# A two-block transformer kernel: table sets named ahead of ScalarE's loops, logarithms and exponentials grouped, experts' transposes in transpose mode

## What is computed

```
def rmsnorm(x, g):
    return x * rsqrt(mean(x * x, -1) + EPS) * g

# first block: norm, projection, two chunked scans over both directions (GLA and mLSTM), then
gla_o = head_rmsnorm(gla_h, g1) * silu(gg)
ml_o = sigmoid(mo) * head_rmsnorm(ml_h, g2)
x = x + g1x * (concatenate([gla_o, ml_o]) @ w_out)
# hierarchical mixture of experts: 32 experts, 2 per token, rows sorted by expert, blocks of 128 rows
def expert_block(xb, e):
    gate, up = split(xb @ e_w_in[e])            # 1024 -> 2 x 512
    return (silu(gate) * up) @ e_w_out[e]       # 512 -> 1024
x = x + g2x * hier_moe(modulate(rmsnorm(x, norm2_g), sh2x, sc2x))
# second block: two layers of mixers (HGRN2 scan, dilated windows, RWKV7), twice a convolved GLU FFN,
# a gated embedding: sigmoid(rmsnorm(h) @ ple_gate) * ..., a last norm
q = silu(q_raw); f = lb + (1 - lb) * sigmoid(f_raw); log_f = log(f)     # HGRN2
```

## Time and profile before

| | before |
|---|---|
| median of 3 runs | 5431.38 us (5431.25 to 5441.96) |
| profiled execution: span | 5435.4 us |
| around the span | the runs' median is 4.0 us below it |
| TensorE busy, matmuls | 4075.4 us, 75% |
| VectorE busy | 2548.6 us, 47% |
| ScalarE busy | 1390.1 us, 26% |
| GpSimd busy | 113.4 us, 2% |
| DMA | 603.89 MB, mean 111 GB/s |
| experts' stage | 878.27 us of the span |

### The profile page before, as it was taken

How to read it: one execution, slowest core, us unless ns; L and a number is a source line. 1 busy time by engine, 2 the same in 40 slices (tenths; PEclk the granted TensorE clock), 3 DMA queues, 4 the chain that set the end, 5 groups by cost and what they waited for, 6 DMA issues and landing times. The chain is left out here.

```text
span 5435.4 us, 55977 instructions
## 1 busy us (share of the span) xinstructions
PE 4075.4 (75%) x18901; PEld 3193.1 (59%) x18902; DVE 2548.6 (47%) x3659; ACT 1390.1 (26%) x1865; POOL 113.4 (2%) x188
## 2 busy tenths in 40 slices
PE   7698811689774998888479844563897779899877
PEld 2487711568553777766358733441785557777756
DVE  1211156446532745777421146656443357567543
ACT  0401021210213755777320021112002032001022
POOL 0000000000001000000100000000000000000000
PEclk9899955877786999999689977676777889999989
DMA  6132114323362856888323210012001122222211
GB/s 245 54 93 79 55 50 135 108 74 96 127 232 107 316 195 233 312 317 310 110 73 97 81 47 32 24 23 89 26 26 41 46 66 85 83 83 86 83 56 45
DMA packets 438154, 603.89 MB, mean 111 GB/s; under 512 B 50477, under 2 KB 314692, under 8 KB 437828
## 3 DMA queue, kind: packets, MB, share of 16 engines
q1 hardware_dynamic: 370072, 459.47, 25.8%
q10 hardware_dynamic: 51552, 86.52, 4.6%
q0 software_dynamic: 16464, 57.07, 2.8%
HBM read 470.13 MB, written 132.84 MB: 111 GB/s over the span
## 5 line engine op out<-in xcount | busy, mean ns | idle before, releaser
L1577 DVE TENSOR_TENSOR exp_w_lo<-exp_w_raw,exp_w_hi 128x1024 fp32r<-128x1024 f32 x384 | 450.4, 1222 | 174.3 <-ACT exp_w_hi L1551 171.6
L1551 ACT ACTIVATE exp_w_hi<-exp_w_raw 128x1024 fp32r<-128x1024 f32 x384 | 381.9, 1050 | 130.1 <-DMA exp_w_raw<-in_expert_w_in 129.7
L324 PE MATMUL in_ps_psum<-hN_hi,in_wh 128*128 128x512 f32 x768 | 301.3, 392 | 52.1 <-DVE in_wl L318 52.1
L324 PE MATMUL up_ps_psum<-hN_hi,up_wh 128*128 128x512 f32 x704 | 285.7, 406 | 70.9 <-DVE up_wl L318 40.6
L325 PE MATMUL in_ps_psum<-hN_lo,in_wh 128*128 128x512 f32 x768 | 300.9, 392 | 0.0
L326 PE MATMUL in_ps_psum<-hN_hi,in_wl 128*128 128x512 f32 x768 | 300.3, 391 | 0.0
L325 PE MATMUL up_ps_psum<-hN_lo,up_wh 128*128 128x512 f32 x704 | 280.6, 399 | 0.0
L326 PE MATMUL up_ps_psum<-hN_hi,up_wl 128*128 128x512 f32 x704 | 280.2, 398 | 0.0
L324 PE MATMUL exp_up_psum<-exp_w_hi,exp_x_hi 128*128 128x512 f32 x592 | 241.8, 409 | 35.3 <-DVE exp_w_lo L1577 34.9
L316 DVE CAST in_wh<-in_w 128x1024 fp32r<-128x1024 f32 x48 | 33.3, 695 | 461.6 <-PE in_ps_psum L326 450.5
L325 PE MATMUL exp_up_psum<-exp_w_lo,exp_x_hi 128*128 128x512 f32 x592 | 232.4, 392 | 0.0
(11 more groups left out here) (653 smaller groups left out, 9129.5 us busy)
## 6 DMA issues: line engine op xcount, KB each, us to landing
exp_w_raw<-in_expert_w_in SPq DMA_DIRECT2D x256, 512.0 KB, 5.1
exp_w_raw<-in_expert_w_out SPq DMA_DIRECT2D x128, 512.0 KB, 5.8
up_w<-in_ffn_up SPq DMA_DIRECT2D x88, 512.0 KB
moe_rows<-zero_rows ACTq DMA_DIRECT2D x50, 512.0 KB, 2.7
ada_w<-in_ada_w SPq DMA_DIRECT2D x12, 2048.0 KB, 7.8
in_w<-in_w_in SPq DMA_DIRECT2D x48, 512.0 KB, 4.0
down_w<-in_ffn_down SPq DMA_DIRECT2D x44, 512.0 KB
exp_rows<-moe_rows POOLq DMA_DIRECT2D x39, 512.0 KB, 6.2
```

Of the source, the lines that this page charges most:

```text
L324: pe.matmul(out, r(w[0]), r(x[0]), start=start, stop=False)
L1551: act.activation(wh[:, c, :].bitcast(F32R), raw[r][:], ACT.Copy).then_inc(s_wh, 1)
L1577: dve.tensor_tensor(wl[:, c, :].bitcast(F32R), raw[r][:], wh[:, c, :], ALU.subtract).then_inc(s_wl[r], 1)
```

## The change

Three things:

- `act.preload_act_table_set(name)` is written ahead of ScalarE's loops (and of the groups of logarithms and exponentials), and names the one set that the loop uses: silu for conv, experts and the up projection, exp for gla, sigmoid for the embedding, and for the gates and hgrn a set that has both Ln and Exp.
- In `stage_norm`, `stage_join` and the RWKV exit all logarithms come first and then all exponentials, where before each Ln was followed by its Exp. In the two-part join VectorE's adds of a part are issued together, ahead of that part's products. Semaphore targets follow.
- In `stage_experts` the turns of the rows and of `h` are `pe.transpose` and no longer `pe.matmul` against the identity.

```
--- before.py
+++ after.py
@@ -354,11 +354,13 @@
                         if n >= NB:
                             act.wait_ge(s_used, n - NB + 1)
                         act.activation(sq[n % NB][:], at(src, h, k), ACT.Square).then_inc(s_sq, 1)
+                act.preload_act_table_set("natural_log")
                 for h in range(nh):
-
                     act.wait_ge(s_used, 8 * h + 8)
                     act.activation(rstd[h][:], pm[h][:], ACT.Ln, bias=K.c("eps")).then_inc(s_rt, 1)
-                    act.wait_ge(s_rt, 2 * h + 1)
+                act.preload_act_table_set("exp_and_others")
+                for h in range(nh):
+                    act.wait_ge(s_rt, nh)
                     act.activation(rstd[h][:], rstd[h][:], ACT.Exp, scale=-0.5).then_inc(s_rt, 1)
                     for k in range(8):
                         n = 8 * h + k + 1
@@ -395,7 +397,7 @@
                 for n in range(8 * nh):
                     h, k = n // 8, n % 8
                     if k == 0:
-                        dve.wait_ge(s_rt, 2 * h + 2)
+                        dve.wait_ge(s_rt, nh + h + 1)
                     if parts and n >= NB:
                         dve.wait_ge(s_lo, n - NB + 1)
                     if shift is not None:
@@ -745,6 +747,7 @@
 
             @block.scalar
             def _(act):
+                act.preload_act_table_set("natural_log_exp_and_others")
                 act.wait_ge(s_lb, NCH)
                 act.activation(le[:], lx[:], ACT.Abs).then_inc(s_a, 1)
                 act.wait_ge(s_a, 1)
@@ -828,6 +831,7 @@
 
             @block.scalar
             def _(act):
+                act.preload_act_table_set("silu_and_others")
                 with act.Fori(0, D // P // NU) as i:
                     for u in U:
                         act.wait_ge(s_tap[u], (i + 1) * NTAP)
@@ -1178,10 +1183,12 @@
                     dve.tensor_tensor(a[u][:], a[u][:], b[u][:], ALU.add).then_inc(s_x[u], 1)
                 heads = [(r, u) for r in range(len(parts)) for u in U]
                 if two:
-                    add(0, 0)
+                    for u in U:
+                        add(0, u)
                 for n, (r, u) in enumerate(heads):
-                    if two and n + 1 < len(heads):
-                        add(*heads[n + 1])
+                    if two and u == 0 and r:
+                        for v in U:
+                            add(r, v)
                     dve.wait_ge(s_a[u], r * 3 + 3)
                     step = Count(dve, s_v[u], r * 2)
                     step(dve.scalar_tensor_tensor(rs[u][:], rs[u][:], K.col(parts[r][1], u), g[u][:], ALU.mult, ALU.mult))
@@ -1190,16 +1197,23 @@
             @block.scalar
             def _(act):
                 for r in range(len(parts)):
+                    steps = [Count(act, s_a[u], r * 3) for u in U]
+                    act.preload_act_table_set("natural_log")
                     for u in U:
                         if two:
                             act.wait_ge(s_x[u], r + 1)
                         else:
                             act.wait_ge(s_in[u], (r + 1) * nin)
-                        step = Count(act, s_a[u], r * 3)
-                        step.mark(act.activation(sq[u][:], a[u][:], ACT.Square))
+                        steps[u].mark(act.activation(sq[u][:], a[u][:], ACT.Square))
+                    for u in U:
                         act.wait_ge(s_mm[u], r + 1)
-                        step(act.activation(rs[u][:], pm[u][:].rearrange("p a b -> p (a b)"), ACT.Ln, bias=K.c("eps")))
-                        step.mark(act.activation(rs[u][:], rs[u][:], ACT.Exp, scale=-0.5))
+                        if r:
+                            act.wait_ge(s_v[u], r * 2)
+                        steps[u].mark(act.activation(rs[u][:], pm[u][:].rearrange("p a b -> p (a b)"), ACT.Ln, bias=K.c("eps")))
+                    act.preload_act_table_set("exp_and_others")
+                    for u in U:
+                        act.wait_ge(s_a[u], r * 3 + 2)
+                        steps[u].mark(act.activation(rs[u][:], rs[u][:], ACT.Exp, scale=-0.5))
 
             @block.tensor
             def _(pe):
@@ -1489,7 +1503,7 @@
                 def turn(b):
                     pe.wait_ge(s_x, b * 16 + 16)
                     for k in range(KT):
-                        mm = pe.matmul(pt[:, k, :], xr[:, k * P:(k + 1) * P], K.c("ident"), start=True, stop=True)
+                        mm = pe.transpose(pt[:, k, :], xr[:, k * P:(k + 1) * P], K.c("ident"))
                     mm.then_inc(s_t, 1)
 
                 for n in U:
@@ -1512,7 +1526,7 @@
                             pe.wait_ge(s_h, b * 2 + (n + 1))
                             for k in range(KE // 2):
                                 f = slice(n * (DE // 2) + k * P, n * (DE // 2) + (k + 1) * P)
-                                mm = pe.matmul(ph[n][:, k * BR:(k + 1) * BR], h[:, f], K.c("ident"), start=True, stop=True)
+                                mm = pe.transpose(ph[n][:, k * BR:(k + 1) * BR], h[:, f], K.c("ident"))
                             mm.then_inc(s_ht, 1)
                         pe.wait_ge(s_ye, b + 1)
                         for c in range(KT, NW):
@@ -2377,7 +2393,9 @@
                 for u in U:
                     act.wait_ge(s_mm, 3 + u)
                     act.activation(rs[u][:], flat(pv[u][:]), ACT.Ln, bias=K.c("gn_eps")).then_inc(s_a, 1)
-                    act.wait_ge(s_a, 3 + 2 * u)
+                act.preload_act_table_set("exp_and_others")
+                for u in U:
+                    act.wait_ge(s_a, 4)
                     act.activation(rs[u][:], rs[u][:], ACT.Exp, scale=-0.5).then_inc(s_a, 1)
 
             @block.vector
@@ -2388,7 +2406,7 @@
                 for u in U:
                     step = Count(dve, s_v, 2 + u * NV)
                     dve.wait_ge(s_mm, 3 + u)
-                    dve.wait_ge(s_a, 4 + 2 * u)
+                    dve.wait_ge(s_a, 5 + u)
                     step(dve.scalar_tensor_tensor(y[u][:], y[u][:], K.col("rwkv_ln_w_2", u), rs[u][:], ALU.mult, ALU.mult))
                     step(dve.scalar_tensor_tensor(y[u][:], y[u][:], K.col("rwkv_ln_b_2", u), K.rk_bonus[:, u, :], ALU.add, ALU.add))
                     step(dve.tensor_tensor(mixF[:, tile + u, :], y[u][:], K.rk_gate[:, u, :], ALU.mult))
@@ -2655,6 +2674,7 @@
 
             @block.scalar
             def _(act):
+                act.preload_act_table_set("sigmoid_and_others")
                 with act.Fori(0, KT // 2) as i:
                     for u in U:
                         act.wait_ge(s_mm[u], i + 1)
```

10 lines of the change are left out of this document (8 added, 2 removed).

## The result

The changed kernel takes 5349.84 us (median of 4 runs, 5343.73 to 5357.06) against 5431.32 us for the kernel before (5425.30 to 5441.96): ratio 0.984, 95% interval 0.9821 to 0.9859. The prediction was 5341 us, with a range of 5324 to 5382. The profiled execution has a span of 5342.2 us, 93.2 us less than before; my sum made it 5345. It is the fastest of the four; the runs' median is 7.6 us above that span.

What follows compares the result with a forecast made beforehand. TensorE works 75% of the span and ScalarE 26%, so table loads matter only where somebody waits. Experts 52.6, norms 6.1, joins 19.9, gates 6.5 and hgrn 5.2 sum to 90.3 us saved: 5341 us, range 5324 to 5382.

Steps and rivals of the forecast that it cites:

- the ring: Experts' repeating cycle, from one expert's first weight copy to the next one's: 23.57 us, forecast to become 21.9 us.
- L1551's load: Table load before each expert's first weight copy; nothing covers it, so its removal saves 32 x 1.30 = 41.6 us.
- the further blocks: Experts' five blocks beyond one per expert: table load and h's turn save 5 x 1.5 = 7.5 us.
- What takes it back: Experts' transfers, squeezed into a shorter ring, take back 0.25 us per expert, 8 us; bounds 0 and 1.6 us per expert.
- The first wait for a tile: ScalarE's wait ahead of an expert's second four weight copies: 2.2 us before, 2.5 forecast, near 3.8 in (a).
- (a): Rival: transfers hold the experts' ring, so only the further blocks and first turn gain, 9 us; 5385 us, chance 0.13.
- The transposes: Experts: h's turn saves 0.3 us per expert, 9.6 us; rows' turn hidden with one block; first turn saves 1.9 us.
- rival (c): The 33.9 us of issue ahead of L1551's loads belong to them and go with them; 5307 us, chance 0.04.
- Norms: Logarithms first: five norms gain 1.8 us each, nf1 and no lose 2.9 us together, n1c unchanged; together -6.1 us.
- Joins: Grouped Ln and Exp shorten join1 by 9.8 us and join2 by 10.1 us; bounds 15 and 22 for both.
- (b): Rival: the set name does not carry through loops and loads come back at their heads; 5388 us, chance 0.07.
- (d): Rival: transposes fail to keep TensorE's clock up, matmuls behind them run at half clock; 5521 us at 15 blocks, chance 0.04.

Runs made afterwards that it cites:

- e7: Changed kernel with two table loads, exp then silu, put ahead of each expert's first weight copy; one run of 5401.38 us.
- e9: Changed kernel with ScalarE's and VectorE's reads of the experts' block table moved between the fourth and fifth weight tile; 5313.67 us, ratio 0.9778.
- e12: Kernel before, loads and plain transposes kept, with only the block table reads moved behind the fourth weight tile; 5406.68 us, ratio 0.9952.
- e8: Changed kernel without the experts' store of y and its waits; one run of 5318.96 us.
- e1: Kernel before with only the experts' two turns, of the rows and of h, in transpose mode; 5413.25 us, ratio 0.997.
- e5: Changed kernel with the rows' turn a plain matmul again, h's turn still in transpose mode; 5349.91 us, ratio 0.9851.
- e3: Kernel before with all of the change except its three edits in the experts; 5398.21 us, ratio 0.9943.
- e4: The changed kernel unaltered, run and profiled a second time; 5349.10 us, ratio 0.9847.

## Why the prediction was right, point by point

The result lies 9 us above the prediction: the medians differ by 81.5 us, where the sum has 90.3. The profiled executions differ by 93.2, and that they agree so well is in part luck. The one before lies 4 us above its runs' median, the one after 8 us below, and hgrn before, 317.3 us, is the longest of the four without its edit. Inside the sum, errors cancel: too little was put down for what the ring gives back, and too little for the transposes and for hgrn. The mechanism held, a load at the ring's restart with nobody to hide it; the sizes of some terms did not.

- **L1551's load, 41.6 us.** The price of 1.30 us is shown (e7: 1.29 us for each of two). The set alone shortened the stage by 35 us, where the sum has 40 for it (41.6 and 6.4 for the further blocks, less 8). Of the whole stage the sum has 52.6 us, and the two profiles give 48.2 and 41.2.
- **What takes it back, 0.25 us of the ring.** This is the term that I mis-sized. It is 0.55 us: h comes at 18.46 and not at 17.91, about 18 us over the stage and not 8. It hangs on the eighth tile, which lands at 11.66 and not at 11.11. In the changed kernel 0.36 of it is VectorE's restart behind x_lo (first subtraction at 2.68 for 2.32), so that SyncE sends the tile later, and the rest is the tile's way. I had not asked what the next late engine was once ScalarE started sooner. But the two are not independent: e9 takes VectorE's delay away and h stays, e12 has 0.27 us without it. The first wait for a tile, which I had named as the sign for this term, was the wrong one: it grew to 3.37 us on average, between the 2.5 of my sum and the 3.8 of (a), and e8 brought it back to 2.72 without moving h.
- **The transposes.** 0.3 us at h's turn was 0.38 in the changed kernel (from h to the end of h_hi, 2.05 to 1.67 us). Transposes alone gave 20 us in the stage for 12.5, because ScalarE's second read of the block table fell at another place beside y's store and took 0.41 us for 0.82 (e1, e8). The hiding of the rows' turn held (e5).
- **The 33.9 us of issue, rival (c).** I gave it to the loop's registers and branches, and that was right in the main: 1.08 us a ring beside the load, it stayed at 0.85 to 1.01 us when the load went, and it holds the two reads. But I took it for a constant. e9 and e12 show that it could be removed by itself, for 23 us alone and 30 to 37 us without the load.
- **Norms, -6.1.** The step is shown: the first Exp 1.49 us late, the second 1.9 sooner, nf1 and no longer by 1.6 and 1.9. The measured -12.5 had 1.7 us of clock in each of n2, nf and np on top; e3 has them without it.
- **Joins, -19.9 against -21.4; gates -6.5 against -6.4; hgrn -5.2 against -7.7** over all profiles. In hgrn's second round VectorE is 1.28 us earlier up to its 25th us, which is the load, and 3.7 us earlier in the second half, where it waits for TensorE at another phase of the granted clock.
- **Rivals.** (a) and (b) fell: the ring moved, and no load came back. (d), the clock, was right in that shortened turns make it fall more often (23 dips with them alone, 4 to 7 with plain turns), and its sign, a clock under 0.95, did appear (0.93 in e1, 0.94 in e4); it was wrong in its price. Whether it is the mode or only the shorter time that TensorE is busy, no run separates. In the changed kernel 25 of the 29 rings have a stretch at 0.50 in them and take 21.96 us on average, the other four 21.95: the up product ends at 16.2 us, and h is not due before 18.46. With the ring at its shortest this is less sure: in e9 it is 21.08 us against 20.76, with only four rings on the one side.

## What to carry to other kernels

A table load, or any instruction at the point where a loop restarts, is worth its own length less what the other engines and the transfers are late by behind it: write down for each engine when it could start the next round, before taking the first one's delay away. Reads of a loop's bounds into registers stand in the ring like work and belong where the engine waits anyway. Where two functions are in one set, naming that set beats grouping: grouping delayed the first result by 1.5 us a norm, and the one set needs no order at all.

## What the runs showed that was not expected

A read of the block table into ScalarE's registers shows in the timeline only as "issue", and that gap ahead of a ring's first copy varied from 0.58 to 1.17 us on average from kernel to kernel, load taken off, with the same instructions in it. It is the two reads (0.28 us each without y's store beside them, up to 1.4 with it) and 0.70 us of other instructions, less the 0.61 to 0.80 us by which the first read starts ahead of x_hi's end. TensorE's granted clock dipped for 3.4 us at a time in a stage that is 86% matmul (716 of 830 us), and more often when eight transposes took half the time. A stage of unchanged code (mlstm) took between 315.6 and 332.7 us, the shortest at a mean granted clock of 0.755 and the longest at 0.722.
